# A hybrid decoder step: v's store earlier in SyncE's list, gate weights loaded first, fewer filler products, five low parts on GpSimd

## The reference

```python
xn = rmsnorm(h, norm_mix)
z = xn @ w_in                                   # 1024 -> 3592 columns
conv_out, new_a = causal_dwconv(z[C] * z[H], buf_a, conv_a_w)
y_a = z[B] * conv_out
qkv, new_qkv = causal_dwconv(z[QKV], buf_qkv, conv_qkv_w)
q, k, v = split(silu(qkv)); q, k = l2norm(q) * dk**-0.5, l2norm(k)
g = -exp(a_log) * softplus(z[A] + dt_bias); beta = sigmoid(z[BETA])   # the gate columns
o, S = gated_delta_chunked(q, k, v, g, beta, S)  # per chunk: triangular solve, then
#   v_new = u - w S; o = q_dec S + qk v_new; S = S exp(g_last) + k_dec^T v_new
o = rmsnorm(o, gdn_norm) * silu(gate)
h = h + concat(y_a, o) @ w_out
u = relu(rmsnorm(h, norm_ffn) @ w_up); h = h + (u * u) @ w_down
y = rmsnorm(h, norm_final)
```

## Time and profile before

| | us |
|---|---|
| median of 3 runs | 1348.75 (1348.11 to 1349.98) |
| the profiled execution | 1350.52 |
| span of its instructions | 1348.7 |
| TensorE busy | 1323.9 |
| VectorE busy | 832.0 |
| GpSimd busy | 523.2 |
| ScalarE busy | 411.3 |
| mean granted TensorE clock | 0.992 |

### The profile page before, as it was taken

The page is one execution under the profiler, slowest core; times in us unless marked ns, Lnnn a source line. Parts: engine busy times, 40 slices in busy tenths (PEclk is TensorE's granted clock), DMA queues, the critical chain, the costliest instruction groups (busy, mean ns, idle before and its releaser), DMA issues.

```text
span 1348.7 us, 22568 instructions
## 1 busy us (share of the span) xinstructions
PE 1323.9 (98%) x9049; PEld 1293.7 (96%) x9049; DVE 832.0 (62%) x1406; ACT 411.3 (30%) x805; POOL 523.2 (39%) x544
## 2 busy tenths in 40 slices
PE   6999999999999999999999999999999999999997
PEld 5999999799999999999999999999999999999997
DVE  4466799324564646556675666666667567566855
ACT  6566652112222213222132222322222223223312
POOL 1322112111211211122267467574674765746811
PEclk9999999899999999999999999999999999999999
DMA  6122561743322213321111111112012021111212
GB/s 191 48 69 69 165 197 36 172 151 89 86 79 79 80 55 88 96 79 34 47 47 48 48 39 57 48 48 63 32 50 61 34 63 47 48 48 46 71 42 114
DMA packets 161850, 99.88 MB, mean 74 GB/s; under 512 B 19639, under 2 KB 156371, under 8 KB 161746
## 3 DMA queue, kind: packets, MB, share of 16 engines
q1 hardware_dynamic: 138770, 85.56, 21.6%
q10 hardware_dynamic: 22976, 12.88, 3.5%
HBM read 77.62 MB, written 20.80 MB: 73 GB/s over the span
## 4 chain that ended last, share of the span: by engine, by line
PE 95%; DVE 3%; DMA 1%; ACT 0%; issue 0%; SPq 0%; POOL 0%; ACTq 0%; DVEq 0%
PE banks L1345 10%; PE banks L1347 10%; PE banks L1346 10%; PE banks L1856 9%; PE banks L1858 9%; PE banks L1857 9%; PE banks L1875 7%; PE banks L1876 7%; PE banks L1874 7%; PE banks L1890 1%; PE banks L1891 1%; PE banks L1892 1%; PE banks L1552 1%; PE banks L1566 1%; PE banks L1786 1%; PE banks L1468 1%
## 5 line engine op out<-in xcount | busy, mean ns | idle before, releaser
L1856 PE MATMUL banks<-hg_high,w_high 128*128 128x384 f32 (+1 forms) x768 | 249.5, 325 | 0.0
L1858 PE MATMUL banks<-hg_high,w_low 128*128 128x384 f32 (+1 forms) x768 | 247.6, 322 | 0.0
L1857 PE MATMUL banks<-hg_low,w_high 128*128 128x384 f32 (+1 forms) x768 | 247.4, 322 | 0.0
L2553 DVE TENSOR_TENSOR hT<-hT,banks 128x528 f32<-128x528 f32 x280 | 189.5, 702 | 84.3 <-PE banks L1876 73.0
L1345 PE MATMUL banks<-xn_high,w_high 128*128 128x384 f32 (+1 forms) x672 | 228.5, 340 | 2.0 <-DVE w_low L1959 1.6
L1346 PE MATMUL banks<-xn_low,w_high 128*128 128x384 f32 (+1 forms) x672 | 219.5, 327 | 0.0
L1347 PE MATMUL banks<-xn_high,w_low 128*128 128x384 f32 (+1 forms) x672 | 219.5, 327 | 0.0
L786 POOL TENSOR_TENSOR w_low<-w_raw,w_high 128x1024 fp32r<-128x1024 f32 x31 | 77.0, 2484 | 249.6 <-ACT w_high L981 249.6
L1856 PEld LDWEIGHTS banks<-hg_high,w_high 128*128 128x128 f32 x768 | 144.2, 188 | 1.9 <-POOL w_low L913 1.7
L1857 PEld LDWEIGHTS banks<-hg_low,w_high 128*128 128x128 f32 x768 | 144.3, 188 | 0.1
L1858 PEld LDWEIGHTS banks<-hg_high,w_low 128*128 128x128 f32 x768 | 144.2, 188 | 0.0
(11 more groups left out here) (321 smaller groups left out, 2787.0 us busy)
## 6 DMA issues: line engine op xcount, KB each, us to landing
w_raw<-in_w_up SPq DMA_DIRECT2D x32, 512.0 KB, 4.0
w_pair<-in_w_down SPq DMA_DIRECT2D x32, 512.0 KB, 3.4
w_raw<-in_w_in SPq DMA_DIRECT2D x28, 512.0 KB, 4.3
w_raw<-in_w_out SPq DMA_DIRECT2D x8, 512.0 KB, 4.2
x_slice<-in_x_prompt SPq DMA_DIRECT2D x8, 512.0 KB, 4.1
out<-y_tok SPq DMA_DIRECT2D x8, 512.0 KB, 2.6
x_tok<-in_x_prompt SPq DMA_DIRECT2D x2, 1536.0 KB, 11.9
v_kept_rows<-v_feat SPq DMA_DIRECT2D x4, 536.0 KB, 5.8
```

What stands on the lines that cost most here:

```text
L1856: pe.matmul(bank[:, 0:w], w_h[half][:, k, :], hg_h[:, k, c0:c0 + w], start=(k == 0), stop=False)
L1857: pe.matmul(bank[:, 0:w], w_h[half][:, k, :], hg_l[:, k, c0:c0 + w], start=False, stop=False)
L1858: ins = pe.matmul(bank[:, 0:w], w_l[half][:, k, :], hg_h[:, k, c0:c0 + w], start=False, stop=(k == KT - 1))
L2553: dve.tensor_tensor(hc, hc, both, ALU.add if sign > 0 else ALU.subtract).then_inc(acc_read_dve, 1)
```

## The change

Five edits in the lists of the engines. SyncE stores a v head at g == 1 of the unit after it, before load(n) instead of behind it. The load of the gate columns (ab_raw) is issued directly behind the first weight tile, ahead of token tiles 3 to 8. ScalarE rounds the gate columns right behind the first weight tile, and GpSimd makes their low part behind the third power. IDLE_PRODUCTS is 3, 1, 1, and VectorE makes w_low of tile 0 ahead of the first xn_low. GpSimd makes the low parts of tiles 10 to 14 at the head of its own list of each tile, and decays the sample states of heads 0 and 1 at unit 37 and of heads 2 and 3 at unit 40.

```diff
--- before.py
+++ after.py
@@ -497,7 +497,7 @@
 
         SQUARE_AFTER = {7: (3, 4, 5, 6), 8: (7,), 10: (8,)}
         AB_AFTER = 9
-        IDLE_PRODUCTS = (6, 4, 2)
+        IDLE_PRODUCTS = (3, 1, 1)
         TURN_AHEAD = 5
 
         def turn_bank(g, k):
@@ -548,7 +548,6 @@
         SOLVE = {29: 3, 30: 3, 31: 3, 32: 3, 33: 3, 34: 3, 35: 3, 36: 5, 37: 5}
         TILE0 = {"k": 30, "w": 35, "sample": (36, 37), "v": 39, "use": 40, "next": 41, "states": 42, "turn": 46, "gate": 50}
         FIRST_ROUND, NEXT_ROUND, STEPS = 42, 47, 5
-        LOW_BY_DVE = range(9, 14)
         LAST_PREPARED = NEXT_ROUND + STEPS * (NT - 2) - 1
         LAST_LAST = 12
         TURN_H = {57: 17, 67: 20, 77: 23, 82: 26}
@@ -674,7 +673,7 @@
                         sp.dma_start(SSs[h // 2][:, h % 2, :, :], ssm_v[:, h, :, :]).then_inc(s_states, 16)
                     sp.wait_ge(y0_sent, 16)
                     sp.dma_start(h3(Y0[:, :]), kept_tile0(Y0_d)).then_inc(y0_load, 16)
-                if g == 2 and n >= 9 and IN_TILES[n - 1][0] == "v":
+                if g == 1 and n >= 9 and IN_TILES[n - 1][0] == "v":
                     h = IN_TILES[n - 1][1]
                     sp.wait_ge(silu_done, n)
                     sp.dma_start(v_d[h], vf[:, h, :]).then_inc(v_sent, 16)
@@ -708,9 +707,9 @@
                     step(3 * (n - 3) + 1)
                 load(n)
                 if n == 0:
+                    sp.dma_start(ab_raw[:, :, :], w_in_v[:, :, O_A:O_A + 8]).then_inc(s_ahead, 16)
                     sp.dma_start(x_big[:, 2:5, :], xp_v[:, 2:5, :]).then_inc(s_xin[3], 16)
                     sp.dma_start(x_big[:, 5:8, :], xp_v[:, 5:8, :]).then_inc(s_xin[4], 16)
-                    sp.dma_start(ab_raw[:, :, :], w_in_v[:, :, O_A:O_A + 8]).then_inc(s_ahead, 16)
                     sp.wait_ge(s_xin[3], 16)
                     sp.dma_start(rows_q[0:24, :], state_conv_qkv.rearrange("l b r c -> (l b r) c")).then_inc(s_row, 16)
                     sp.dma_start(rows_q[24:28, :], conv_qkv_w[0]).then_inc(s_row, 16)
@@ -786,13 +785,12 @@
                 pool.tensor_tensor(w_l[n % 2][:, :, :], w_raw[n % 2][:, :, :], w_h[n % 2][:, :, :].bitcast(F32),
                                    ALU.subtract).then_inc(w_low, 1)
 
-            for t in GTILES[0] + GTILES[1]:
+            for t in range(NT):
                 x_power(t)
-            pool.wait_ge(ab_hi, 1)
-            pool.tensor_tensor(ab_w[:, :, 8:16], ab_raw[:, :, :], ab_w[:, :, 0:8].bitcast(F32),
-                               ALU.subtract).then_inc(ab_lo, 1)
-            for t in GTILES[2]:
-                x_power(t)
+                if t == 2:
+                    pool.wait_ge(ab_hi, 1)
+                    pool.tensor_tensor(ab_w[:, :, 8:16], ab_raw[:, :, :], ab_w[:, :, 0:8].bitcast(F32),
+                                       ALU.subtract).then_inc(ab_lo, 1)
 
             def history(n):
 
@@ -885,15 +883,18 @@
                     identities()
                 if kind == "H":
                     history_a(i)
-                if n not in LOW_BY_DVE:
+                if n + 1 < N_MIX:
                     split_low(n + 1)
                 for u in range(3 * n, 3 * n + 3):
                     t, s = round_step(u)
                     if u == TILE0["k"]:
                         beside()
+                    if u == TILE0["sample"][-1]:
+                        decay_states(0)
+                        decay_states(1)
                     if u == TILE0["use"]:
-                        for h in range(NH):
-                            decay_states(h)
+                        decay_states(2)
+                        decay_states(3)
                     if u == TILE0["states"]:
                         power(0)
                     if s == 3 and t >= 2:
@@ -997,6 +998,8 @@
             for t in GTILES[0]:
                 square_x(t)
             split_high(0)
+            act.wait_ge(s_ahead, 16)
+            act.activation(ab_w[:, :, 0:8], ab_raw[:, :, :], ACT.Copy).then_inc(ab_hi, 1)
             act.wait_ge(rows_kept, 1)
             for m in range(3 * KT):
                 g, k = m // KT, m % KT
@@ -1006,9 +1009,6 @@
                                scale=tn[:, k:k + 1]).then_inc(x_high, 1)
                 for t in SQUARE_AFTER.get(m, ()):
                     square_x(t)
-                    if t == 4:
-                        act.wait_ge(s_ahead, 16)
-                        act.activation(ab_w[:, :, 0:8], ab_raw[:, :, :], ACT.Copy).then_inc(ab_hi, 1)
                 if m == AB_AFTER:
                     keep_ab(0)
             split_high(1)
@@ -1947,6 +1947,9 @@
                     dve.wait_ge(rows_turned, 1)
                     dve.tensor_copy(tn[:, :], ps[0][:, 0:16]).then_inc(rows_kept, 1)
                 scale_x(t)
+            dve.wait_ge(w_high, 1)
+            dve.tensor_tensor(w_l[0][:, :, :], w_raw[0][:, :, :], w_h[0][:, :, :].bitcast(F32),
+                              ALU.subtract).then_inc(w_low, 1)
             for m in range(3 * KT):
                 g, k = m // KT, m % KT
                 c0, w = GROUPS[g]
@@ -1954,10 +1957,6 @@
                 dve.scalar_tensor_tensor(out=xl[:, k, c0:c0 + w], in0=ps[turn_bank(g, k)][:, 0:w], scalar=tn[:, k:k + 1],
                                          in1=xh[:, k, c0:c0 + w].bitcast(F32), op0=ALU.mult,
                                          op1=ALU.subtract).then_inc(x_low, 1)
-                if m == 0:
-                    dve.wait_ge(w_high, 1)
-                    dve.tensor_tensor(w_l[0][:, :, :], w_raw[0][:, :, :], w_h[0][:, :, :].bitcast(F32),
-                                      ALU.subtract).then_inc(w_low, 1)
                 if m == KT - 1:
                     mean_x(3)
                     scale_x(3)
@@ -2421,19 +2420,10 @@
                 if s == 5 and t < NT:
                     take_state_of_k(t)
 
-            def split_low(n):
-
-                dve.wait_ge(w_high, n + 1)
-                dve.wait_ge(acc_done, 3 * (n - 1))
-                dve.tensor_tensor(w_l[n % 2][:, :, :], w_raw[n % 2][:, :, :], w_h[n % 2][:, :, :].bitcast(F32),
-                                  ALU.subtract).then_inc(w_low, 1)
-
             for n in range(N_IN):
                 kind, i, _ = IN_TILES[n]
                 for g in range(3):
                     u = 3 * n + g
-                    if g == 1 and n in LOW_BY_DVE:
-                        split_low(n + 1)
                     if kind == "H":
                         evict_h(n, g)
                     if kind == "B" and g:
```

## The result

The changed kernel takes 1351.34 us (median of 22 runs, 1350.37 to 1356.79), the kernel before 1347.52 us (22 runs, 1345.33 to 1353.36): a ratio of 1.0026, 95% interval 1.0016 to 1.0036. It was forecast at 1336.1, so 12.6 us faster; it is 3.8 us slower by the medians. Its profiled execution took 1353.07 us with a span of 1351.2. Beside the experiments, executions of the kernel before took 1345.54 to 1348.65 us at a mean granted clock of 0.994 to 0.996, or 1349.65 to 1353.31 us at 0.992; its profiled one (1350.52, 0.992) belongs with the second.

A forecast was written before the change was run, and what follows sets the result against it. TensorE, working 98% of the span, was taken as the bound. Opening 5.3, v_meta wait 2.8, clock behind it 4.8, less 0.3 for low parts: 12.6 us saved, 1336.1 us median (1337.9 profiled); range 1333.3 to 1342.5.

The forecast's parts named there:

- low parts on GpSimd: Five low parts moved off VectorE: each blocks VectorE up to 2.3 us, gives back 1.22; 0.3 us cost in the sum.
- Rival A: At next_state0: the clock is low there all the same; 4.8 us fall away, 7.8 saved, 1340.9; chance 0.15.
- rival B: Opening gives half: clock doubles later or a low stretch follows the new gap; costs 1.7 to 2.5, 1338.3; chance 0.12.
- rival C: Solve is the bound: Y store late, TensorE waits 3 us at tile 1's first level; 5 less, 1341; chance 0.07.
- Opening: Program start: less filler, sooner w_low[0] and gate weights; first dense step at 12.5 instead of 15.84, 5.3 us gained.
- v's store: Ahead of next_state0: sooner store removes 2.8 us of wait for v_meta and 4.8 us of half clock behind it.
- Solve and Y store: Solve ends near 239.5 instead of 234.6; Y store lands about 247.2, ScalarE wants it at 248.6; cost taken as 0.
- The lock: GpSimd subtractions exclude VectorE instructions with two SBUF inputs; all five low parts block, the sum unchanged, only the slack.

The follow-up runs named there:

- e6_late_w: Kernel before with silu(10) on ScalarE moved right ahead of keep_w0 in unit 35, VectorE and GpSimd untouched; 1360.08 us, ratio 1.0093.
- e5_open_vstore: Kernel before with the opening's edits and v's store a unit sooner, low parts and decays as before; 1338.04 us, ratio 0.9926.
- e1: Kernel before with the opening's edits alone (filler 3, 1, 1; gate weights first; w_low[0] ahead of xn_low[0]); 1345.88 us, ratio 0.9985.
- e4_silu_behind: Changed kernel with ScalarE's silu of the third v head moved behind keep_w0 of unit 35; 1342.22 us, ratio 0.9960 to the kernel before.
- e9_steps_first: Changed kernel with TensorE's order changed in unit 36: three dense steps before the first three parts of the sample products; 1342.04 us, ratio 0.9956.
- e3_pool_low: Kernel before with only the five low parts and the decays changed on GpSimd; 1356.92 us, ratio 1.0069.
- e10_bunched: Changed kernel with the sample products of units 36 and 37 behind all eight dense steps of each unit; 1341.92 us, ratio 0.9958.

## Why the prediction was wrong

**The step that failed** is "The ends for this edit are 0 (TensorE waited for none of this work before) and a loss of 2", of the low parts on GpSimd. Measured, this edit costs 9.7 us alone and 13.3 on top of the other two. A slower kernel had got a chance of 0.03. VectorE's lateness was about as reckoned: by the prediction's own terms three blocks and two subtractions given back make 1.5 + 2 x 2.3 - 2 x 1.22 = 3.7 us at the third v head, and silu of that head starts 0.9 us before unit 36 in the changed kernel against 4.1 before it in the kernel before, 3.2 us later. (The 3.5 us of the text is the sum for four low parts, at the end of the solve.) It was followed to VectorE's own consumers (the solve, v_meta, keep_rows), not into ScalarE's list, where one silu that waits for VectorE holds back an instruction that has nothing to do with it. "TensorE waited for none of this work" was true and proved little: ScalarE finished keep_w0 at 210.64 and TensorE's first sample product started at 210.78. The slack was at most 0.14 us.

**Second, the price of a wait.** Rival A put a low clock at next_state0, rival B in the opening, rival C behind a level of tile 1. None had it at the sample products, where it lasts longest, and the three were priced at 1.7 to 5 us. The fall there cost about 13.6 us: 11.4 while the sample products ran (25.5 for 14.1) and the rest behind them. That is near the 12.9 us of e6_late_w and the 13.3 us between the changed kernel and e5_open_vstore.

**Opening.** Right in kind: no wait for the gate products, the second group started by scaled tiles, and no low clock behind the short waits there (0.55 and 0.87 us). Its profile gained 3.9 of 5.3 us; the first dense step came at 14.45 instead of the forecast 12.5. I had the clock rise at the same time as before; in this execution it rose at about 14.2, and in e1 and e5 at 12.2 and 11.6. That is the mechanism of rival B; with TensorE's later start it took 1.4 us. With filler 3, 1, 1 the rise came at 11.4 or later in all eight profiled executions, with 6, 4, 2 at 8.9, 9.1, 9.6, 11.2 and 14.7 in five; whether the count or chance decides is open. TensorE's start at 6.06 instead of 5.57 is the constants' DMA. In medians the edit is worth 1.3 us alone. The wait for v_meta takes 1.3 us back (2.8 became 4.1); where the rest of the 4.4 us went is open.

**v's store.** Right in mechanism, including the clock behind next_state0, where the equally small products at full clock were the right row to go by. Its size, 7.6 us, was read from one execution, the one with the longest low stretch at this place; the median gives 4.2.

**Solve and Y store.** Rival C named the wait for At, and e4_silu_behind and e9_steps_first show it, 2.3 and 2.2 us, once the sample stage is at full speed. The sum had it at 0. It put the end of the solve 4.9 us later; the Y store of e4_silu_behind is issued 6.7 us later than that of e5_open_vstore, whose opening and v store are the same.

**The lock.** What the Trainium skill states on its page "SBUF — State Buffer", section "Who interferes with whom", held: the trace agrees, with 2.31 and 2.48 us for solve steps of 0.25 and 0.37 us. The page says who blocks whom; that only slack would change was my step, not the page's.

## What to carry to other kernels

When an engine is made later by some us, follow every instruction list that waits for it, and for each wait found ask what stands behind the waiting instruction and how much slack that has. A wait of half a microsecond on TensorE has no fixed price: look at the work behind it. Here, next to small products, it put 27 us at half the clock and cost 13 us. Moving work to another engine also moves it in time: reckoned from TensorE's work, GpSimd's third low part came some 9 us sooner than VectorE's own had, so that up to the third v head three blocks stood against two subtractions given back. Where such a wait cannot be removed, give TensorE some dense steps first, or move the one instruction that holds back another engine's queue.

## What the runs showed of the hardware

Waits of 0.5 to 0.6 us ahead of products of 8 columns interleaved with dense steps were followed by 27 to 31 us at 1.2 GHz in three kernels (27 in the changed one and in e6_late_w, 31 in e3_pool_low), while the same interleaved work without a wait ran at 2.4 GHz in the others (before, e1, e4, e5 and e9 are shown or told above). The low level ended only when dense steps came alone. In e10_bunched, with the products apart, it ended after 3.4 us, and there it had come without any idle time of TensorE. At the start of the program the clock rose between 8.9 and 14.7 us in different executions, under filler of 3, 1, 1 or 6, 4, 2 products. A GpSimd subtraction of 128x1024 (2.4 to 3.3 us) held up VectorE instructions with two SBUF inputs: 0.25 us became 2.31 and 0.37 became 2.48, while a VectorE instruction that reads PSUM (L2171, four in 1.11 us) kept its time beside one.
